# Two-block transformer kernel: one weight transfer behind the last shifted rows, mean sums split around the last taps, 64-column products in pairs, own rows read in runs

## Chip, cores and metric

The kernel runs on one core of a Trainium2 chip, as one program launched once. The metric is the time of one execution in microseconds (us), the median over several runs. The engines of the core are TensorE (PE, matrix products; its weight loads are PEld), VectorE (DVE), ScalarE (ACT), GpSimd (POOL) and SyncE (SP, which here only issues DMAs; POOL issues the indirect ones).

## The reference

The input x has 512 tokens of 1024 features. A first block has two layers, each a mixer and a convolutional FFN around residuals; the second layer's mixer is `conformer_conv`. A second block has a hybrid of attention and a state-space branch, a cross attention on a memory, and a mixture of 64 experts (8 per token) with a shared expert. What the change touches:

```python
def conformer_conv(x, pw1_w, pw1_b, dw_w, dw_b, ln_g, ln_b, pw2_w, pw2_b):
    h = jax.nn.glu(x @ pw1_w + pw1_b, axis=-1)
    h = causal_dwconv(h, dw_w, dw_b)             # 31 taps, each channel by itself
    h = jax.nn.silu(layer_norm(h, ln_g, ln_b))
    return h @ pw2_w + pw2_b

h_q, h_kv, k_rope_raw, u, g_mla, g_s5 = jnp.split(x @ w_in, IN_OFFSETS, axis=-1)
k_rope = apply_rope(k_rope_raw, cos, sin)        # 32 columns of w_in

scores = jax.nn.sigmoid((x2d @ w_router).astype(jnp.float32))   # 1024 -> 64 experts
...
return routed + swiglu(x2d, w_sh_gu, w_sh_down)  # then layer_norm_2(DEEPNORM_ALPHA * x + ff)
```

## The kernel before

Activations lie with features on the 128 partitions, as 8 tiles of 128 features by 512 tokens. Each engine has its own program, written out by hand in order; engines meet at semaphores. Weights come through a ring of two slots (`wring`), which SP fills in the order of its `slot(...)` calls (L745 to L755); one call issues two or three DMAs and waits until PE has used the slot's former content. Large products are split into high and low parts, three products for one (`proj_split`, L1405). Products of plain fp32 operands show in the profile as two PE instructions each.

**Depthwise convolution** (PE's `conv_taps`, L1685 to L1696). Of the 31 taps PE does 20 and DVE 11. For PE, a channel tile must lie in SBUF four times, shifted by 5 columns from one to the next. SP's `shift_rows(j)` (L856 to L864) makes these: one DMA writes the tile to DRAM (`conv_rows`, L858), and when that has landed, four DMAs read it back shifted (L864). For j >= 2 the reads also wait for the taps of tile j-2 (`tap_used`), whose buffer they fill. The 40 PE instructions of one tile (5 steps by 4 strips of 32 channels, 2 each) wait for these reads. The weights of the two pointwise products are six slots (`conv_slots`), issued between the tiles:

```python
for j in range(NK):
    shift_rows(j)
    if j % 2 == 0:
        slot(*conv_slots[2 + j // 2])
```

The layer norm behind it sums over features with a matrix of ones: `layer_norm` (L1491) adds the eight tiles into one PSUM bank, each once DVE has added its own taps (`conv_taken`); then `sum_squares` (L1473) does the same for the squares. DVE takes the mean at L3024. `keep_clock(n)` (L1353) issues n small products that nothing uses.

**Key product.** `tile` (L1361) multiplies the 64 columns `wkr` (the 32 rope key columns and the same ones turned for the rotation) with the 8 feature tiles; DVE multiplies by cosine and sine (L3507, `take_key`), and `spread_key` (L1755) adds the halves and repeats the key with a matrix `wrep` that POOL builds from the identity (L1201).

**Router.** After the second norm ACT writes the 8 tiles of `hT` (L2698), PE multiplies each with its 64 columns `wrt` (L2034), ACT copies the logits (L2798), and PE turns them to tokens on partitions (L2042). DVE's routing runs up to L3799, and PE's `positions` (L2053 to L2056) waits for its result. DVE also splits the shared expert's weights (`shared_lo`, L3750) and its inputs (L3761, L3762).

**Own rows.** The shared expert's down product goes to eight PSUM tiles of 128 tokens by 512 features. `own_row(i)` (L2153) first copies the tokens' residual rows there, as a product with the identity; `row_tok` holds a row with features in the order (k, q), and the tile wants (q, k). The first four `own_row` stand at the head, then `shared_down` (L2160 to L2162) with `m_idx` (L2084, an expert's token list) between, then the last four, one ahead of each further `shared_down`. DVE makes indices of the lists, POOL gathers the tokens of the first experts (L1279), and SP issues the first down weights of the experts (L1027) once the second gather has landed.

**Experts.** Per expert PE does 24 gate/up products (L2105 to L2107), transposes (L2093, L2115) and 12 down products (L2127 to L2129). ACT makes the high parts of the weights (gate/up L2836, down L2843) and DVE the low ones. SP loads three experts ahead, each load behind PE's last use of its buffer. The functions, as they were:

Of the kernel before, what the change touches and what calls it, by code (L numbers as in the profile page):

```python
# [28 lines left out]
ALU = mybir.AluOpType  # L29
ACT = mybir.ActivationFunctionType  # L30
AX = mybir.AxisListType

P = 128
T = 512
D = 1024
NK = D // P
# [113 lines left out]
def build(nc, A, out):  # L150

    ctx = ExitStack()
    with ctx:
# [73 lines left out]
        def align():  # L227

            top[0] = -(-top[0] // LINE) * LINE
# [337 lines left out]
        sc_c2 = carve(4 + 64)  # L567
        ranks = carve(TC * NE)
        align()
        sact_hi.append(carve_r(T)[1])  # L570
# [171 lines left out]
        def _(sp):  # L742
# [127 lines left out]
            for j in range(NK):  # L870
                shift_rows(j)
                if j % 2 == 0:
                    slot(*conv_slots[2 + j // 2])
            ffn(1)
# [251 lines left out]
        def _(pool):  # L1126
# [71 lines left out]
            pool.wait_ge(tile_done, IN_TILES)  # L1198
            for k in range(2):
                r = slice(32 * k, 32 * k + 32)  # L1200
                link(G.tensor_copy(wrep[r, :].rearrange("p (a b) -> p a b", b=32), ident[r, r].unsqueeze(1).broadcast_to([32, 4, 32])))  # L1201
# [128 lines left out]
        def _(pe):  # L1330
# [24 lines left out]
            def tile(mms, lo=0, hi=P, n=T):  # L1355
# [7 lines left out]
                tiles.inc()  # L1363

            def turn(srcs):

                b = tp[tiles.s % NBANK]
                if tiles.s >= NBANK:
                    pe.wait_ge(tile_evac, tiles.v - NBANK + 1)
                for k, src in enumerate(srcs):  # L1370
                    m = src.shape[0]
                    n = src.shape[1]
                    ins = nc.tensor.transpose(b[0:n, k * P:k * P + m], src, ident[0:m, 0:m])
                ins.then_inc(tile_done, 1)
                tiles.inc()
# [114 lines left out]

            def layer_norm(k, src, centred_sq):  # L1491
                for kk in range(k):
                    pe.wait_ge(conv_taken, kk + 1)
                    ins = nc.tensor.matmul(mp[0][:], ones[:], src[:, kk, :], start=kk == 0, stop=kk == k - 1)
                ins.then_inc(stat_ready, 1)
                nstat.inc()
                sum_squares(k, centred_sq, 1)

# [206 lines left out]
            for s in range(1, 4):  # L1705
                proj_split(NK, u_hi, u_lo, whi, (0, 2, 1, 3), each=lambda t: conv_between(s, t))
            conv_taps(NK - 2)
            conv_taps(NK - 1)
            layer_norm(NK, cv, lnsq)
            keep_clock(30)  # L1710
# [41 lines left out]
            def spread_key():  # L1752
                pe.wait_ge(key_turned, SINCE["key_turned"] + 1)
                pe.wait_ge(qstd, 2)
                nc.tensor.matmul(mp[1][:], wrep[0:64, :], turns[0:64, :], start=True, stop=True).then_inc(key_spread, 1)  # L1755

# [17 lines left out]
            pe.wait_ge(h_ready, NK)  # L1774
            tile([(wkr[:, k, :], hT[:, k, :]) for k in range(NK)], hi=64)
            for n in range(2):
# [254 lines left out]
            pe.wait_ge(in3, 16 * 4)  # L2031
            for k in range(NK):
                pe.wait_ge(h_ready, 3 * NK + k + 1)
                ins = nc.tensor.matmul(mp[2][0:NE, :], wrt[:, k, :], hT[:, k, :], start=k == 0, stop=k == NK - 1)  # L2034
            ins.then_inc(rt["logits"], 1)
            for c in range(TC):
                for half in range(2):
                    turn([hT[:, 4 * half + k, c * P:(c + 1) * P] for k in range(4)])
                if c == 0:
                    pe.wait_ge(rt["weights_hi"], 4 + 1)  # L2040
                    for c1 in range(TC):
                        ins = nc.tensor.matmul(mp[0][:, c1 * NE:(c1 + 1) * NE], logit_rows[0:NE, c1 * P:(c1 + 1) * P],  # L2042
                                               ident[0:NE, 0:NE], start=True, stop=True)
                    ins.then_inc(rt["logits"], 1)
# [108 lines left out]
            def own_row(i):  # L2153
                pe.wait_ge(tile_evac, RES_TILES - 8 + i - NBANK + 1)
                by_feature = row_tok[i // 2].rearrange("p (k q) -> p q k", k=NK)
                nc.tensor.matmul(down_bank(i), ident[:], by_feature[:, 64 * (i % 2):64 * (i % 2) + 64, :], start=True, stop=False)

# [80 lines left out]
        def _(act):  # L2238
# [558 lines left out]
            act.wait_ge(rt["logits"], 1)  # L2797
            nc.scalar.activation(logit_rows[0:NE, :], mp[2][0:NE, :], ACT.Copy).then_inc(rt["weights_hi"], 1)  # L2798
            act.wait_ge(rt["logits"], 2)
# [140 lines left out]
        def _(dve):  # L2940
# [562 lines left out]
            def take_key():  # L3503
                dve.wait_ge(sin_ready, 2)
                link(V.tensor_scalar(rope, rope, sc_consts[:, 1:2], None, ALU.mult))
                dve.wait_ge(tile_done, tiles.v + 1)
                link(V.tensor_tensor(turns[0:64, :], tp[tiles.s % NBANK][0:64, :], rope[0:64, :], ALU.mult))  # L3507
                dve.nop().then_inc(tile_evac, 1)
                dve.nop().then_inc(key_turned, 1)
                tiles.inc()  # L3510
# [236 lines left out]
            def shared_lo(c):  # L3747
# [3 lines left out]
                 .then_inc(rt["weights"], 1)  # L3751

            shared_lo(0)
            shared_lo(1)
# [295 lines left out]
```

## Time and profile before

| | us |
| --- | --- |
| median of 3 runs | 2661.35 (2660.39 to 2661.96) |
| the profiled execution | 2660.82 |
| its span in the trace | 2659.1 |
| PE busy | 2573.0 |
| DVE busy | 1922.9 |
| ACT busy | 1348.0 |
| POOL busy | 310.4 |

Times in the views count from the start of the span. A row of the timeline gives the start, the duration, the engine, the line of the kernel, the operation, output and inputs with their shapes, the number of instructions merged, and in brackets the idle time ahead of them with what ended it. The mean of PE's granted clock over the span is 0.992 of full speed.

### The profile page before, as it was taken

How to read it: one execution, taken by the hardware profiler on the slowest of the kernel's cores; microseconds unless marked ns; L12 is line 12 of the kernel's file. 1: busy time of each engine (PE TensorE's matmuls, PEld its weight loads, DVE VectorE, ACT ScalarE, POOL GpSimd, SP SyncE). 2: the span in 40 equal slices, each digit the busy share in tenths (PEclk: the TensorE clock that was granted, in tenths of full speed). 3: DMA queues.
4: the chain of work that ended last, by engine and by line, in shares of the span. 5: the costliest groups of instructions: out<-in, count | busy, mean ns of one | idle time of the engine just before them, and what ended most of it. 6: DMA issues, size and time to landing. Idle time of an engine off the chain costs nothing.

```text
span 2659.1 us, 34694 instructions
## 1 busy us (share of the span) xinstructions
PE 2573.0 (97%) x12396; PEld 1985.4 (75%) x12396; DVE 1922.9 (72%) x2762; ACT 1348.0 (51%) x1968; POOL 310.4 (12%) x270
## 2 busy tenths in 40 slices
PE   8999999999999989999999999999999999999996
PEld 7888878788887647888887765586667777777773
DVE  4788765677835856778637637465588999999996
ACT  4766652222323225222334233444457888998883
POOL 0000000100000010000002600000026622222220
PEclk9999999999999999999999999999999999999998
DMA  3222232222233651222233560323139999999996
GB/s 113 72 64 70 64 103 95 97 95 95 92 92 102 182 93 66 95 95 95 87 96 123 154 146 17 102 90 132 48 133 370 398 397 391 400 397 397 391 390 274
DMA packets 266488, 446.25 MB, mean 168 GB/s; under 512 B 46527, under 2 KB 200200, under 8 KB 241540
## 3 DMA queue, kind: packets, MB, share of 16 engines
q1 hardware_dynamic: 247555, 408.38, 43.9%
q0 software_dynamic: 18816, 36.35, 4.5%
q8 instruction: 70, 1.15, 0.2%
q14 instruction: 47, 0.38, 0.0%
HBM read 424.90 MB, written 44.84 MB: 177 GB/s over the span
## 4 chain that ended last, share of the span: by engine, by line
PE 87%; DVE 5%; DMA 3%; ACT 3%; issue 1%; SPq 1%; DVEq 0%; ACTq 0%
PE tp L1405 41%; PE tp L2105 4%; PE tp L2107 4%; PE tp L2106 4%; PE tp L1511 3%; PE tp L1513 3%; PE tp L1512 3%; PE tp L1361 2%; PE mp L2129 2%; PE mp L2127 2%; PE mp L2128 2%; PE tp L2093 2%; PE tp L1452 2%; PE mp L1694 1%; PE tp L1903 1%; DMA uT<-in_w_exp_gu 1%
## 5 line engine op out<-in xcount | busy, mean ns | idle before, releaser
L1405 PE MATMUL tp<-sq_r,arena_r 128*128 128x512 f32 x1056 | 414.3, 392 | 5.8 <-DVE uT_r L2986 3.5
L1405 PE MATMUL tp<-uT_r,arena_r 128*128 128x512 f32 x1056 | 411.9, 390 | 0.0
L1405 PE MATMUL tp<-sq_r,wring_r 128*128 128x512 f32 x1056 | 411.7, 390 | 0.0
L1405 PEld LDWEIGHTS tp<-sq_r,arena_r 128*128 128x128 f32 x1056 | 198.6, 188 | 55.1 <-issue 11.7
L1405 PEld LDWEIGHTS tp<-sq_r,wring_r 128*128 128x128 f32 x1056 | 198.7, 188 | 41.5
L1405 PEld LDWEIGHTS tp<-uT_r,arena_r 128*128 128x128 f32 x1056 | 198.7, 188 | 40.8 <-issue 0.5
L2958 DVE TENSOR_TENSOR wring_r<-wring,arena_r 128x2048 fp32r<-128x2048 f32 x82 | 187.2, 2322 | 50.1 <-ACT arena_r L2268 49.9
L1405 PE MATMUL tp<-arena_r,wring_r 128*128 128x512 f32 x564 | 219.5, 389 | 0.0
L2268 ACT ACTIVATE arena_r<-wring 128x2048 fp32r<-128x2048 f32 x82 | 152.2, 1903 | 52.4 <-DMA wring<-in_b_pw_w 21.9
L2511 ACT ACTIVATE arena<-arena 128x512 f32<-128x512 f32 x44 | 27.8, 632 | 288.1 <-DVE arena L3044 288.0
L3895 DVE TENSOR_TENSOR arena_r<-arena,arena_r 128x1024 fp32r<-128x1024 f32 x128 | 150.5, 1217 | 0.5 <-ACT arena_r L2843 0.5
L3044 DVE SCALAR_TENSOR_TENSOR arena<-lead,pcol,arena 128x512 f32<-128x512 f32 x176 | 132.4, 752 | 20.7 <-DVE arena L3044 4.9
L1405 PE MATMUL tp<-arena_r,sq_r 128*128 128x512 f32 x436 | 134.5, 390 | 0.0
L1405 PE MATMUL tp<-arena_r,uT_r 128*128 128x512 f32 x436 | 134.4, 390 | 0.0
L2255 ACT ACTIVATE lead<-tp 128x512 f32<-128x512 f32 x70 | 41.1, 597 | 175.7 <-PE tp L1405 126.2
L1511 PE MATMUL tp<-sq_r,wring_r 128*128 128x512 f32 x320 | 128.4, 401 | 0.9 <-DVE wring_r L3094 0.9
L2843 ACT ACTIVATE arena_r<-arena 128x1024 fp32r<-128x1024 f32 x128 | 127.8, 1049 | 0.0
L1513 PE MATMUL tp<-sq_r,wring_r 128*128 128x512 f32 x320 | 124.9, 390 | 0.0
L1512 PE MATMUL tp<-uT_r,wring_r 128*128 128x512 f32 x320 | 124.6, 389 | 0.0
L1405 PEld LDWEIGHTS tp<-arena_r,wring_r 128*128 128x128 f32 x564 | 105.9, 188 | 22.2
L2105 PE MATMUL tp<-hT_r,arena_r 128*112 128x512 f32 x256 | 103.1, 403 | 0.0
L3040 DVE TENSOR_TENSOR lead<-tp,rinv 128x512 f32<-128x512 f32 x88 | 60.6, 688 | 58.0 <-PE tp L1405 57.7
(625 smaller groups left out, 5950.3 us busy)
## 6 DMA issues: line engine op xcount, KB each, us to landing
wring<-in_w_exp_gu SPq DMA_DIRECT2D x64, 1024.0 KB, 14.5
arena<-in_w_exp_down SPq DMA_DIRECT2D x64, 1024.0 KB, 22.6
uT<-in_w_exp_gu SPq DMA_DIRECT2D x32, 1024.0 KB, 14.9
sq<-in_w_exp_gu SPq DMA_DIRECT2D x32, 1024.0 KB, 14.8
wring<-in_f_up_w SPq DMA_DIRECT2D x22, 1024.0 KB, 5.0
wring<-in_f_up_w SPq DMA_DIRECT2D x44, 512.0 KB, 6.3
wring<-in_f_down_w SPq DMA_DIRECT2D x32, 448.0 KB, 5.4
wring<-in_a_in_proj SPq DMA_DIRECT2D x42, 256.0 KB, 2.7
```

What stands on the lines that cost most here:

```text
L1405: ins = nc.tensor.matmul(b[:], parts[wp][:, kk, m * P:(m + 1) * P], xparts[xp][:, kk, :], start=n_k == 0 and q == 0, stop=n_k == k - 1 and ...
L1511: nc.tensor.matmul(bank[:], w_hi[:, kk, cs], u_hi[1][:, kk, :], start=kk == 0, stop=False)
L1512: nc.tensor.matmul(bank[:], w_hi[:, kk, cs], u_lo[1][:, kk, :], start=False, stop=False)
L1513: ins = nc.tensor.matmul(bank[:], w_lo[:, kk, cs], u_hi[1][:, kk, :], start=False, stop=kk == NK - 1)
L2105: nc.tensor.matmul(out, x_hi, hi[:, k, :], start=k == 0, stop=False)
L2106: nc.tensor.matmul(out, x_hi, lo[:, k, :], start=False, stop=False)
L2107: ins = nc.tensor.matmul(out, x_lo, hi[:, k, :], start=False, stop=k == NK - 1)
L2268: nc.scalar.activation(hi[r][1][:, a:b], wring[r][:, a:b], ACT.Copy).then_inc(whi_ready, 1)
L2843: nc.scalar.activation(wdn_hi[b][:, s], wdn[q][:, s], ACT.Copy).then_inc(moe["dhi"], 1)
L2958: V.tensor_tensor(wlo[r][:, a:b], wring[r][:, a:b], hi[r][1][:, a:b].bitcast(F32), ALU.subtract).then_inc(wlo_ready, 1)
L3044: ins = V.scalar_tensor_tensor(dst, r[:, PAD - t:PAD - t + T], w(taps - 1 - t), dst, ALU.mult, ALU.add)
L3895: V.tensor_tensor(wdn_lo[q][:, s], wdn[q][:, s], wdn_hi[b][:, s].bitcast(F32), ALU.subtract).then_inc(moe["dlo"], 1)
```

## The change

Four edits:

1. SP issues the last of the six weight slots behind `shift_rows(7)`, not behind `shift_rows(6)`.
2. PE does the first six mean sums between the taps of tile 6 and those of tile 7, and the last two behind those of tile 7.
3. The two products with 64 output columns (key and router) send even feature tiles to PSUM partitions 0 to 63 and odd ones to 64 to 127; the halves are added in what follows: `spread_key` contracts all 128 rows, and the logits' turn uses `two_idents`, two identities of 64 one above the other, which DVE makes. POOL builds four blocks of `wrep` in place of two. PE waits for `two_idents` ahead of the logits' turn.
4. `own_row` reads the residual row in runs of 64 contiguous numbers and writes PSUM in steps of 8 numbers (32 bytes), where it read in steps of 128 numbers (512 bytes) and wrote contiguously.

```diff
             for j in range(NK):
                 shift_rows(j)
-                if j % 2 == 0:
-                    slot(*conv_slots[2 + j // 2])
+                if j in (0, 2, 4, 7):
+                    slot(*conv_slots[2 + {0: 0, 2: 1, 4: 2, 7: 3}[j]])
...
-            for k in range(2):
+            for k in range(4):
                 r = slice(32 * k, 32 * k + 32)
...
+            def paired(bank, w, before):
+
+                for k in range(NK):
+                    before(k)
+                    half = bank[64 * (k % 2):64 * (k % 2) + 64, :]
+                    ins = nc.tensor.matmul(half, w[:, k, :], hT[:, k, :], start=k < 2, stop=k >= NK - 2)
+                return ins
...
-            def layer_norm(k, src, centred_sq):
-                for kk in range(k):
+            def conv_mean(ks):
+                for kk in ks:
                     pe.wait_ge(conv_taken, kk + 1)
-                    ins = nc.tensor.matmul(mp[0][:], ones[:], src[:, kk, :], start=kk == 0, stop=kk == k - 1)
-                ins.then_inc(stat_ready, 1)
-                nstat.inc()
-                sum_squares(k, centred_sq, 1)
+                    ins = nc.tensor.matmul(mp[0][:], ones[:], cv[:, kk, :], start=kk == 0, stop=kk == NK - 1)
+                return ins
...
             conv_taps(NK - 2)
+            conv_mean(range(NK - 2))
             conv_taps(NK - 1)
-            layer_norm(NK, cv, lnsq)
+            conv_mean(range(NK - 2, NK)).then_inc(stat_ready, 1)
+            nstat.inc()
+            sum_squares(NK, lnsq, 1)
...
-                nc.tensor.matmul(mp[1][:], wrep[0:64, :], turns[0:64, :], start=True, stop=True).then_inc(key_spread, 1)
+                nc.tensor.matmul(mp[1][:], wrep, turns, start=True, stop=True).then_inc(key_spread, 1)
...
-            tile([(wkr[:, k, :], hT[:, k, :]) for k in range(NK)], hi=64)
+            pe.wait_ge(tile_evac, tiles.v - NBANK + 1)
+            ins = paired(tp[tiles.s % NBANK], wkr, lambda k: None)
+            ins.then_inc(tile_done, 1)
+            tiles.inc()
...
-            for k in range(NK):
-                pe.wait_ge(h_ready, 3 * NK + k + 1)
-                ins = nc.tensor.matmul(mp[2][0:NE, :], wrt[:, k, :], hT[:, k, :], start=k == 0, stop=k == NK - 1)
-            ins.then_inc(rt["logits"], 1)
+            paired(mp[2], wrt, lambda k: pe.wait_ge(h_ready, 3 * NK + k + 1)).then_inc(rt["logits"], 1)
...
                     pe.wait_ge(rt["weights_hi"], 4 + 1)
+                    pe.wait_ge(rt["weights"], 1)
                     for c1 in range(TC):
-                        ins = nc.tensor.matmul(mp[0][:, c1 * NE:(c1 + 1) * NE], logit_rows[0:NE, c1 * P:(c1 + 1) * P],
-                                               ident[0:NE, 0:NE], start=True, stop=True)
+                        ins = nc.tensor.matmul(mp[0][:, c1 * NE:(c1 + 1) * NE], logit_rows[:, c1 * P:(c1 + 1) * P],
+                                               two_idents, start=True, stop=True)
...
             def own_row(i):
                 pe.wait_ge(tile_evac, RES_TILES - 8 + i - NBANK + 1)
-                by_feature = row_tok[i // 2].rearrange("p (k q) -> p q k", k=NK)
-                nc.tensor.matmul(down_bank(i), ident[:], by_feature[:, 64 * (i % 2):64 * (i % 2) + 64, :], start=True, stop=False)
+                by_slice = row_tok[i // 2].rearrange("p (k q) -> p k q", k=NK)[:, :, 64 * (i % 2):64 * (i % 2) + 64]
+                by_feature = down_bank(i).rearrange("p (q k) -> p k q", k=NK)
+                nc.tensor.matmul(by_feature, ident[:], by_slice, start=True, stop=False)
...
-            nc.scalar.activation(logit_rows[0:NE, :], mp[2][0:NE, :], ACT.Copy).then_inc(rt["weights_hi"], 1)
+            nc.scalar.activation(logit_rows, mp[2][:], ACT.Copy).then_inc(rt["weights_hi"], 1)
...
-                link(V.tensor_tensor(turns[0:64, :], tp[tiles.s % NBANK][0:64, :], rope[0:64, :], ALU.mult))
+                link(V.tensor_tensor(turns, tp[tiles.s % NBANK][:], rope, ALU.mult))
...
+            dve.wait_ge(in3, 16 * 4)
+            link(V.tensor_tensor(two_idents, ident[:, 0:NE], ident[:, NE:P], ALU.add))
             shared_lo(0)
```

On SP, at the last two tiles of the convolution, the order before was this (`conv_rows` is the buffer in DRAM, `arena` holds the shifted copies, `wring` is the ring of weights):

```order
L858 DMA conv_rows<-arena 128x542
L864 DMA arena<-conv_rows 32x4x516 x4
L752 DMA wring<-in_b_pw_w 128x3x512 x2
L752 DMA wring<-in_b_pw_w 128x2x512
L858 DMA conv_rows<-arena 128x542
L864 DMA arena<-conv_rows 32x4x516 x4
```

and now is this, with the three transfers of the last slot behind the reads of tile 7:

```order
L859 DMA conv_rows<-arena 128x542
L865 DMA arena<-conv_rows 32x4x516 x4
L859 DMA conv_rows<-arena 128x542
L865 DMA arena<-conv_rows 32x4x516 x4
L753 DMA wring<-in_b_pw_w 128x3x512 x2
L753 DMA wring<-in_b_pw_w 128x2x512
```

On PE, at the end of the same convolution, before (taps of tiles 5, 6 and 7 in one row, the means, the squares, and the products that nothing uses; a row of `order` counts products, of which the profile shows two instructions each):

```order
L1405 MATMUL tp<-sq_r,wring_r 128x512
L1694 MATMUL mp<-arena 32x512 x60
L1494 MATMUL mp<-arena,ones 128x512 x8
L1473 MATMUL mp<-arena,ones 128x512 x8
L1353 MATMUL mp<-ident 128x128 x30
```

and now, with six of the means ahead of the last 20 taps:

```order
L1414 MATMUL tp<-sq_r,wring_r 128x512
L1701 MATMUL mp<-arena 32x512 x40
L1503 MATMUL mp<-arena,ones 128x512 x6
L1701 MATMUL mp<-arena 32x512 x20
L1503 MATMUL mp<-arena,ones 128x512 x2
L1482 MATMUL mp<-arena,ones 128x512 x8
L1354 MATMUL mp<-ident 128x128 x30
```

On PE, at the first four own rows, before (ahead of them the shared expert's gate/up products, behind them its down products and an expert's list):

```order
L2068 MATMUL tp<-arena_r,wring_r 128x512
L2156 MATMUL tp<-arena,ident 128x512 x4
L2160 MATMUL tp<-hT_r,arena_r 128x512
L2161 MATMUL tp<-wring_r,arena_r 128x512
L2162 MATMUL tp<-hT_r,arena_r 128x512
L2084 MATMUL mp<-arena_r 128x6 x4
```

and now, in the same place, with the other shape of the access:

```order
L2079 MATMUL tp<-arena_r,wring_r 128x512
L2168 MATMUL tp<-arena,ident 128x8x64 x4
L2172 MATMUL tp<-hT_r,arena_r 128x512
L2173 MATMUL tp<-wring_r,arena_r 128x512
L2174 MATMUL tp<-hT_r,arena_r 128x512
L2095 MATMUL mp<-arena_r 128x6 x4
```

## Rows read from the trace of the kernel before

**Rows 1.** The page, first part: busy us, share of the span, instructions.
```profile
PE 2573.0 (97%) x12396; PEld 1985.4 (75%) x12396; DVE 1922.9 (72%) x2762; ACT 1348.0 (51%) x1968; POOL 310.4 (12%) x270
```
**Rows 2.** Chain of waits, 955 to 985 (start, us, what); then DVE's timeline.
```profile
955.09 8.62 DMA conv_rows<-arena
...
965.04 5.49 DMA arena<-conv_rows
...
976.84 7.08 PE mp L1494 x16
...
954.31 0.69 DVE L3342 TENSOR_TENSOR arena<-arena 128x512 f32<-128x512 f32 x1 [5.53 <-ACT arena L2255]
```
**Rows 3.** Timeline of PE at the last taps.
```profile
953.43 8.80 PE L1694 MATMUL mp<-arena 128*32 128x512 f32 x80
970.62 6.22 PE L1694 MATMUL mp<-arena 128*32 128x512 f32 x40 [8.40 <-DMA arena<-conv_rows]
```
**Rows 4.** Window behind the gap: us; busy PE, PEld, DVE, ACT, POOL; clock, DMA share, GB/s.
```profile
971.00:984.00 13.00, 12.90 (x56) 4.40 (x48) 0.75 (x2) 0.00 (x0) 5.53 (x7) 0.88 0.64 1
```
**Rows 5.** DMA issues, 934 to 950, then 950 to 976: KB, median us to landing.
```profile
conv_rows<-arena SPq DMA_DIRECT2D x1, 271.0 KB, 2.1
...
wring<-in_b_pw_w SPq DMA_DIRECT2D x1, 512.0 KB, 7.5
```
**Rows 6.** Timeline of ACT: first use of the moved slot.
```profile
1015.43 3.71 ACT L2268 ACTIVATE arena_r<-wring 128x2048 fp32r<-128x2048 f32 x2
```
**Rows 7.** Timeline of PE at the key product.
```profile
1465.71 7.08 PE L1361 MATMUL tp<-hT,arena 128*64 128x512 f32 x16
```
**Rows 8.** Timeline of POOL, first work behind the copies of L1201.
```profile
1446.69 1.70 POOL L1157 TENSOR_TENSOR arena<-pcol,arena 128x576 f32<-128x576 f32 x1 [37.08 <-ACT arena L2613]
```
**Rows 9.** Timelines of DVE, ACT, PE, DVE and PE at the router.
```profile
1930.76 2.36 DVE L3750 TENSOR_TENSOR wring_r<-wring,arena_r 128x1024 fp32r<-128x1024 f32 x2 [1.64 <-ACT arena_r L2788]
...
1937.88 5.36 ACT L2698 ACTIVATE hT<-sq,pcol 128x512 f32<-128x512 f32 x8 [2.32 <-DVE sq L3017]
...
1938.74 7.05 PE L2034 MATMUL mp<-hT,arena 128*64 128x512 f32 x16 [1.53 <-ACT hT L2698]
...
1963.31 0.29 DVE L3799 TENSOR_SCALAR arena<-arena 128x256 f32<-128x256 f32 x1
...
1963.97 0.33 PE L2054 MATMUL mp<-arena,stri 128*128 128x64 f32 x2
```
**Rows 10.** Chain of waits, 1976 to 2010; then the timelines of POOL and SP.
```profile
1978.18 6.91 PE tp L2156 x8
...
1992.43 1.81 PE tp L2156 x2
...
1995.62 1.73 PE tp L2156 x2
...
1992.34 1.51 POOL L1279 DMA_INDIRECT arena<-xtab,arena  x1 [0.30 <-issue]
...
1996.38 0.80 SPq L1027 DMA_DIRECT2D arena<-in_w_exp_down  x2
```
**Rows 11.** Windows before and in the experts' stage, columns as in rows 4.
```profile
1992.00:1996.30 4.30, 4.30 (x13) 2.10 (x14) 3.28 (x7) 1.20 (x2) 3.61 (x3) 1.00 0.23 65
...
2030.00:2600.00 570.00, 568.91 (x2838) 444.02 (x2837) 539.51 (x652) 500.29 (x727) 174.99 (x136) 1.00 1.02 396
```
**Rows 12.** Timeline of ACT in the experts' stage.
```profile
2419.73 3.90 ACT L2836 ACTIVATE hT_r<-sq 128x1024 fp32r<-128x1024 f32 x4 [1.85 <-DMA sq<-in_w_exp_gu]
```
**Rows 13.** Timeline of PE: one transpose, which comes once per expert.
```profile
2268.59 0.35 PE L2115 MATMUL mp<-ident,std 112*128 112x112 f32 x2
...
2416.00 0.35 PE L2115 MATMUL mp<-ident,std 112*128 112x112 f32 x2
...
2584.63 0.36 PE L2115 MATMUL mp<-ident,std 112*128 112x112 f32 x2
```
**Rows 14.** Chain of waits, 2585 to 2660, behind the last expert.
```profile
2598.99 20.72 DMA wring<-ytab
```

More of the change, by code:

```diff
@@ L568, in build @@
         ranks = carve(TC * NE)
+        two_idents = carve(NE)
         align()
```

## The prediction

> **What bounds the kernel now.** The page's first part [rows 1] comes first: TensorE (PE) is busy for 2573.0 of 2659.1 us. A step is therefore worth something if it takes time off PE's own queue or closes one of PE's few gaps, and work on another engine is worth something where PE, or the last stage, waits for it. Next, the chain of waits around the depthwise convolution [rows 2]: the last channel tile's DMA through DRAM takes 8.62 us, the reads of it end at 970.53 (965.04 + 5.49), and PE's 40 tap instructions begin only then, after 8.40 us of idleness; the mean sums follow and end at 983.92 (976.84 + 7.08), and VectorE (DVE) waits for them [rows 2, 3]. The windows give PE's granted clock behind this gap, from 971 to 984, as 0.88 on average [rows 4]: for a part of the stretch it had the lower of its two levels (1.2 and 2.4 GHz), after 8.4 us in which it did nothing. Third, the stage of the 64 experts. PE looks full there, but so are the DMA engines: 1.02 of their time, 396 GB/s, over 570 us [rows 11]. PE's timeline gives 16 experts in 2416.00 - 2268.59 = 147.41 us, 9.21 each, and the next 18 in 168.63 us, 9.37 each [rows 13]: late in the stage ScalarE (ACT) stands 1.85 us for an expert's weights [rows 12], which it did not earlier. From about 2416 on the transfers set the pace, and behind the last expert the chain is one transfer of 20.72 us [rows 14]. So a microsecond saved on PE just ahead of the experts counts only if it also lets the stream of transfers start earlier. The profiled execution took 2660.82 us; the median, 2661.35, is 0.53 above it, and I add that at the end.
>
> **The convolution's DMA order and its mean sums.** The data for the last tile are ready at 955.00 (954.31 + 0.69 on DVE [rows 2]), and its write is issued at once, but behind two weight transfers of 768 KB and one of 512 KB that SP issued just before. The same write took 2.1 us for the tile before it [rows 5]. With the weights moved behind, it lands at 955.1 + 2.1 = 957.2. The reads overwrite the rows of tile 5, whose taps end half way through the group of 80 instructions, at 953.43 + 4.40 = 957.83 [rows 3]; issued at 957.9, and taking from first issue to last landing what they took before (963.71 to 970.53, 6.8 us), they are in by 964.7.
> PE meanwhile ends the taps of tile 6 at 962.23 and does six of the eight means, 12 of the 16 instructions that take 7.08 us [rows 2]: 5.3 us, to 967.5. That is 2.8 us after the reads have landed. So the taps of tile 7 need no wait, and, with no gap ahead of them, take 4.4 us like those of tiles 5 and 6, not 6.22: to 972.0. Two means (1.8 us) end at 973.8. DVE's sum for tile 7 (0.7 us) lies beside the first of them. 983.9 - 973.8: **10.1 us earlier**, namely 8.4 of gap and 1.8 of slow taps, less 0.1. The moved slot issues three DMAs; they now start near 959.7 and land by about 967.5 (7.5 us [rows 5]). ACT first reads them at 1015.43 [rows 6], so nothing waits. On SP nothing else stands behind them until the FFN's weights.
>
> **The key product.** 16 instructions over 64 output columns take 7.08 us [rows 7], 0.44 each, one behind the other. The pairing puts neighbours on different halves of the array's columns. The taps do that with four strips of 32 columns: 80 instructions in 8.80 us, 0.11 each [rows 3], a quarter of 0.44. Two halves side by side should then give 0.22 each, 3.6 us. **Gain 3.4 us**, all on PE's queue. If they do not run side by side it is 0; nothing added could make it a loss. The sum of the two halves is folded into a product that now contracts 128 rows in place of 64: same number of columns, same time. GpSimd's two additional small copies lie in 37.08 us of idleness [rows 8]: 0.
>
> **The router's logits.** The same pairing on 16 instructions, 7.05 us [rows 9]. But ACT delivers their inputs until 1943.24 (1937.88 + 5.36), so the last pair can end only about 1944.3, 1.5 us earlier. Then DVE decides: its routing operations, which do not depend on this product's early end because the conversions of the inputs stand ahead of them in its queue, end at 1963.60 (1963.31 + 0.29), and PE's position sums wait for them at 1963.97 [rows 9]. PE arrives 1.5 us sooner and waits about 1.2: **gain 0.3 us**. The added sum of two identities on DVE (64 columns) falls into its 1.64 us of idleness ahead of 1930.76 [rows 9]: 0. The weights wait added on PE at the transposes is for that sum, long done.
>
> **The own rows.** Eight products, 16 instructions, copy the tokens' own rows into PSUM: 6.91 us for the first four, 1.81 + 3 x 1.73 for the others [rows 10] (two further groups read 1.73), 13.9 us, 0.86 per instruction, where a 128x512 product with contiguous operands takes 7.08/16 = 0.44. What differs is the read with a step of 512 bytes. The change reads runs of 64 contiguous numbers, and moves the step, 32 bytes, to the PSUM side. No row shows a stepped PSUM write by PE. Bounds: 0.44 as for contiguous operands, and 0.86 or above if the step costs there what it did on the read side. I take 0.44, because the taps and the mean sums, whose reads run without such steps, all stand at PE's streaming rate, and the one slow row has the one stepped read. Then PE saves 3.4 us on the first four and 6.8 us in all.
> The Trainium skill speaks against this: "PSUM — Partial Sum Buffer", section "Specifications (TRN2)", says that any non-contiguous access pattern there slows matmuls significantly, in cachelines of 8 bytes. By it the edit saves nothing and the time is that of the second rival below; no run shown here has such a write.
> What reaches the end is less. The expert indices and the gathers depend on the first four own rows alone; the gather of expert 1 is issued by GpSimd at 1992.34, and SP issues the first down weights behind its landing, 1996.38 [rows 10]. These move by 3.3 us; the DMA engines stand nearly idle there (share 0.23 from 1992 to 1996.3 [rows 11]). From then on they are full to the end, their work is unchanged, and the end follows them. **Gain 3.3 us**; the other 3.5 us come back as waits for weights, earlier in the stage than 2416.
>
> **Sum.** 10.1 + 3.4 + 0.3 + 3.3 = 17.1 us; 2660.82 - 17.1 = 2643.7, and with 0.53 the forecast is **2644.2 us**. A measurement of this kernel can tell about 0.2% (5.3 us) from no change.
>
> **Rivals.**
> 1. *The transfers keep up.* If a longer lead of PE only lengthens the queue of loads (their landing has grown without stopping PE until 2416), all 6.8 us count: 20.6 in all, 2640.8. Against it: 9.37 us an expert and ACT's waits at the end [rows 12, 13]. Chance 0.09.
> 2. *The step is as dear in PSUM as in SBUF.* The own rows stay at 0.86 and the other three give 13.8: 2660.82 - 13.8 + 0.53 = 2647.6. Every value between 0.44 and 0.86 lies between this and the forecast. For it: one stepped operand doubled the time in the row before. Chance 0.27.
> 3. *The pairs do not run side by side, or the reads of the last tile come late.* The first costs 3.4 + 0.3 (2647.9), the second what the reads land after 967.5: one more conflict like the 6.5 us that the write lost now would make it 3.7 us, 2647.9. The taps' 0.11 speaks against the one and the 2.8 us of slack against the other. Chance 0.09 together.
> 4. *The stepped PSUM write is far dearer*, the case on the slower side. With e us more per instruction than 0.86, PE is later by 16e and the transfers by 8e; PE has some 2.9 us in hand (18 x 0.16 us lost to the transfers). The gains are gone when 16e - 2.9 = 13.8, e = 1.04, 1.9 us per instruction, over four times a contiguous one. At 2.4 us (e = 1.54) it is 2660.82 - 13.8 + 21.7 + 0.53 = 2669.3. Nothing shows such a price. Chance 0.02 for slower by over 0.2%, and 0.05 for a price between, which leaves the time within 0.2%.
>
> **The numbers.** The forecast's own case has 0.48, with 1.5 us to either side for the windows that I read and the spread of the runs. The range takes in rivals 1 to 3, from 2640 to 2650; what is left out is rival 4 and two mishaps at once. Faster by over 0.2% means under 2656.0: cases 1 to 3 and the forecast, 0.93; within, 0.05; slower, 0.02.
>
> **What would show it.** Right: taps of tile 7 with no DMA wait and 4.4 us long, ahead of the last four mean instructions, and DVE taking the mean about 10 us sooner; 16 key instructions in about 3.6 us; logits ending about 1 us after ACT's last input and a new PE wait for DVE ahead of the position sums; own rows at 0.44; the down weights about 3.3 us sooner against the own rows' start, and ACT's waits for expert weights beginning well before 2350. Wrong: own rows at 0.86 or more (rival 2 or 4); 9.21 us an expert to the end (rival 1); a DMA wait still ahead of the last taps, or 0.44 a key instruction (rival 3).

## The result, and the profile after

| | before | changed |
| --- | --- | --- |
| median of 4 runs, us | 2661.65 | 2645.76 |
| lowest and highest, us | 2660.39, 2662.07 | 2645.16, 2646.24 |
| the profiled execution, us | 2660.82 | 2646.24 |
| its span, us | 2659.1 | 2644.5 |

The ratio is 0.9942, with a 95% interval of 0.9928 to 0.9956: 15.9 us faster by the medians, 14.6 us by the two profiled executions. The forecast was 2644.2 us, 17.1 us faster, in a range from 2640 to 2650. Of all runs below, one of e2_pairs took 3544.77 us at a mean granted clock of 0.68, and its median is that of its other ten.

The page's first part answers to [rows 1]; PE has lost 7.9 us of work:

```profile
PE 2565.1 (97%) x12396; PEld 1984.6 (75%) x12396; DVE 1921.5 (73%) x2763; ACT 1347.8 (51%) x1968; POOL 307.0 (12%) x272
```

PE's timeline at the end of the convolution, with DVE's step that takes the mean as the last line ([rows 2, 3]), and that step in the kernel before:

```profile
954.15 8.80 PE L1701 MATMUL mp<-arena 128*32 128x512 f32 x80
962.88 5.42 PE L1503 MATMUL mp<-arena,ones 128*128 128x512 f32 x12
968.23 4.50 PE L1701 MATMUL mp<-arena 128*32 128x512 f32 x40
972.66 2.00 PE L1503 MATMUL mp<-arena,ones 128*128 128x512 f32 x4
...
974.70 0.69 DVE L3036 TENSOR_SCALAR rinv<-mp 128x512 f32<-128x512 f32 x1 [1.22 <-PE mp L1503]
```
```profile
983.94 0.69 DVE L3024 TENSOR_SCALAR rinv<-mp 128x512 f32<-128x512 f32 x1 [6.35 <-PE mp L1494]
```

The last taps (x40) carry no bracket: they wait for nothing, and take 4.50 us where they took 6.22. The mean is taken 974.70 - 954.15 = 20.55 us behind the start of the group of 80, before 983.94 - 953.43 = 30.51.

What stands behind it is less good. PE's sums of squares, now and in the kernel before, and the windows there and ahead of the key product now (columns as in [rows 4]):

```profile
976.83 8.83 PE L1482 MATMUL mp<-arena,ones 128*128 128x512 f32 x16 [2.17 <-ACT arena L2332]
```
```profile
986.08 7.13 PE L1473 MATMUL mp<-arena,ones 128*128 128x512 f32 x16 [2.17 <-ACT arena L2320]
```
```profile
973.00:990.00 17.00, 14.83 (x61) 8.48 (x60) 9.62 (x12) 8.10 (x11) 5.53 (x7) 0.90 0.97 9
1450.00:1456.00 6.00, 4.24 (x16) 3.70 (x17) 5.97 (x5) 2.80 (x7) 5.84 (x3) 0.72 0.44 141
```

The same 16 instructions took 7.13 us in the kernel before, behind the same wait of 2.17 us, at a granted clock of 1.00. Here the clock was at its lower level (1.2 GHz of 2.4) for a part of each of the two stretches.

The key product, the router's logits and PE's wait ahead of the position sums ([rows 7, 9]):

```profile
1459.91 3.65 PE L1371 MATMUL tp<-hT,arena 128*64 128x512 f32 x16
...
1928.85 5.62 PE L1371 MATMUL mp<-hT,arena 128*64 128x512 f32 x16 [1.53 <-ACT hT L2710]
...
1953.75 0.43 PE L2065 MATMUL mp<-arena,stri 128*128 128x64 f32 x2 [1.13 <-DVE arena L3813]
```

The own rows in the chain of waits, and from the timelines of POOL and SP the second gather and the first down weights ([rows 10]):

```profile
1968.06 3.43 PE tp L2168 x8
...
1978.82 0.96 PE tp L2168 x2
...
1981.16 0.86 PE tp L2168 x2
```
```profile
1978.74 1.50 POOL L1280 DMA_INDIRECT arena<-xtab,arena  x1 [0.30 <-issue]
...
1984.30 0.80 SPq L1028 DMA_DIRECT2D arena<-in_w_exp_down  x2
```

Eight instructions in 3.43 us are 0.43 each. The experts' stage, a window, ACT's timeline and PE's transpose once per expert ([rows 11 to 13]), and ACT's first wait for weights in the kernel before:

```profile
2030.00:2580.00 550.00, 548.32 (x2722) 425.56 (x2721) 517.39 (x622) 483.36 (x703) 158.08 (x128) 1.00 1.02 396
```
```profile
2207.78 3.91 ACT L2848 ACTIVATE arena_r<-uT 128x1024 fp32r<-128x1024 f32 x4 [0.67 <-DMA uT<-in_w_exp_gu]
...
2233.12 0.35 PE L2126 MATMUL mp<-ident,std 112*128 112x112 f32 x2
...
2571.05 0.35 PE L2126 MATMUL mp<-ident,std 112*128 112x112 f32 x2
```
```profile
2353.49 3.91 ACT L2836 ACTIVATE arena_r<-wring 128x1024 fp32r<-128x1024 f32 x4 [0.35 <-DMA wring<-in_w_exp_gu]
```

The DMA engines move the same 396 GB/s. Apart from one wait of 1.09 us at 2028.85, ACT waits for an expert's weights from 2207.78 on, where the first such wait before stood at 2353.49. From 2233.12 the pace is lost: 36 experts in 337.93 us, 9.39 each, where [rows 13] has 9.21 up to 2416.

### The profile page after: what moved, and what is told of

Its sections match the earlier page's. It is cut to its first block, busy times and chain, and to the rows that moved or that the text cites. A ratio compares the mean times of both kernels' runs of the same rounds, so it can differ in the third digit from the quotient of the medians.

```text
span 2644.5 us, 34699 instructions
## 1 busy us (share of the span) xinstructions
PE 2565.1 (97%) x12396; PEld 1984.6 (75%) x12396; DVE 1921.5 (73%) x2763; ACT 1347.8 (51%) x1968; POOL 307.0 (12%) x272
## 4 chain that ended last, share of the span: by engine, by line
PE 86%; DVE 5%; DMA 4%; ACT 2%; SPq 1%; issue 1%; DVEq 0%; ACTq 0%; POOLq 0%
PE tp L1414 41%; PE tp L2116 4%; PE tp L2118 4%; PE tp L2117 4%; PE tp L1518 3%; PE tp L1520 3%; PE tp L1519 3%; PE tp L1362 2%; DMA uT<-in_w_exp_gu 2%; PE mp L2140 2%; PE mp L2138 2%; PE mp L2139 2%; PE tp L1461 2%; PE tp L2104 1%; PE mp L1701 1%; PE tp L1916 1%
```

## The experiments

All were timed beside the kernel before, whose medians in the three series were 2660.18, 2660.12 and 2660.38 us (21 runs each). A run strays by up to 4 us to either side, so differences between medians under 2 us are not read. The granted clock goes with the straying: of the 63 runs of the kernel before, the 16 with a mean clock of 0.990 or 0.991 average 2662.7 us, the four with 0.994 average 2657.0. The traces tell more, but each is of one execution, and not always a typical one: e6's is the fastest of its eleven runs (2649.85), e4's the second slowest (2659.64), e9's the slowest of five (2642.82), e10's the fastest (2642.94). The table cuts each profiled execution at rows of PE's and DVE's timelines: **A** from the start of the last full group of taps to DVE's mean, **B** from there to DVE's reciprocal behind the sums of squares, **C** from there to the key product, **D** from there to the position sums, **E** from the first own row to the end of the span. What lies ahead of A differs by up to 3.4 us between executions of whatever kernel (the taps start at 950.7 to 954.2). The traces of "before" and "changed", and the median of "changed", are those of the first comparison, whose median before is 2661.65.

| kernel | median, us | A | B | C | D | E |
| --- | --- | --- | --- | --- | --- | --- |
| before | 2660.2 | 30.51 | 10.02 | 471.74 | 498.26 | 681.07 |
| e1_conv | 2649.51 | 20.55 | 11.72 | 473.31 | 497.99 | 679.34 |
| e6_slot | 2654.55 | 23.44 | 10.03 | 471.71 | 498.20 | 679.65 |
| e7_means | 2655.77 | 25.05 | 10.02 | 473.34 | 498.38 | 680.79 |
| e2_pairs | 2657.31 | 30.28 | 11.72 | 473.41 | 494.23 | 679.63 |
| e3_own | 2655.91 | 30.12 | 11.72 | 473.24 | 498.22 | 674.66 |
| e4_first | 2657.71 | 30.26 | 11.72 | 473.28 | 498.12 | 676.95 |
| e5_last | 2658.22 | 30.54 | 10.02 | 471.70 | 498.31 | 677.88 |
| changed | 2645.76 | 20.55 | 11.72 | 473.49 | 493.83 | 676.62 |
| e10_again | 2644.55 | 20.55 | 11.72 | 473.37 | 494.37 | 674.38 |
| e8_fill | 2641.93 | 20.55 | 10.02 | 471.80 | 494.18 | 675.38 |
| e9_down | 2640.92 | 20.55 | 11.72 | 473.39 | 494.14 | 675.91 |
| e11_down0 | 2641.71 | 20.55 | 11.72 | 473.40 | 494.57 | 674.40 |
| e12_best | 2642.65 | 20.55 | 10.03 | 471.80 | 494.55 | 674.83 |

The first comparison read by it: 0.72 ahead of A, -9.96 in A, +1.70 in B, +1.75 in C, -4.43 in D, +0.10 up to the own rows, -4.45 in E: -14.6 us, the difference of the spans. E holds also what stands behind the last expert's activation on ACT, 58.4 to 60.1 us, in which the clock drops as well (0.81 from 2600 to 2659 in the kernel before): 60.1 us in the kernel before and 59.1 in the changed one, so 1.0 of the 4.45 us lies there.

### The parts by themselves

**e1_conv**: the kernel before with the two convolution edits.

```diff
-                if j % 2 == 0:
-                    slot(*conv_slots[2 + j // 2])
+                if j in (0, 2, 4, 7):
+                    slot(*conv_slots[2 + {0: 0, 2: 1, 4: 2, 7: 3}[j]])
...
             conv_taps(NK - 2)
+            conv_mean(range(NK - 2))
             conv_taps(NK - 1)
-            layer_norm(NK, cv, lnsq)
+            conv_mean(range(NK - 2, NK)).then_inc(stat_ready, 1)
```

> The two convolution edits alone (weight slot behind the last shifted rows, six means ahead of the last taps). In the changed kernel DVE takes the mean 974.70 - 954.15 = 20.55 us behind the start of the last full group of taps, before 983.94 - 953.43 = 30.51 us: 9.96 us. Behind it the granted clock was 0.90 from 973 to 990, where the kernel before had 1.00 in the like stretch, and DVE's next step stands only 8.25 us ahead. Theory 1: that slower clock belongs to the edit, because PE now meets its 2.17 us wait for the squares in another state: about 2653.4 us (8.3 faster than 2661.65), and the profile shows a clock under 1.00 behind the mean sums. Rival: it was chance of the one execution: about 2651.7 us (10 faster), clock 1.00 there.

Measured: 2649.51 us, ratio 0.9958 (0.9945 to 0.9972), 10.7 us faster by the medians; the interval holds both sums expected (8.3 and 10), so the time does not tell the theories apart. A is 9.96 us shorter; B and C carry the 1.7 us each, and the window behind the mean sums reads a clock of 0.90:

```profile
969.00:986.00 17.00, 14.83 (x60) 8.27 (x57) 9.30 (x11) 8.10 (x11) 5.53 (x7) 0.90 0.94 9
```

But e2, e3 and e4, whose convolution is that of the kernel before, carry both too (e3's sums of squares below). So the slower clock does not need the edit, and theory 1 falls, though its sign, a clock under 1.00, is there. The one execution of the kernel before that the forecast was read from happened to have neither.

```profile
984.40 8.83 PE L1473 MATMUL mp<-arena,ones 128*128 128x512 f32 x16 [2.17 <-ACT arena L2321]
```

**e2_pairs**: the kernel before with the paired key and router products and what follows them.

```diff
-            tile([(wkr[:, k, :], hT[:, k, :]) for k in range(NK)], hi=64)
+            pe.wait_ge(tile_evac, tiles.v - NBANK + 1)
+            ins = paired(tp[tiles.s % NBANK], wkr, lambda k: None)
...
+            paired(mp[2], wrt, lambda k: pe.wait_ge(h_ready, 3 * NK + k + 1)).then_inc(rt["logits"], 1)
```

> The paired key and router products alone, with the two identities and the 128-row followers. Theory: 7.08 us become 3.65 us at the key, 0.3 us are gained at the router, nothing is given back later: 3.7 us faster, about 2657.9 us. In the changed kernel the 24 products ahead of the key took 6.28 us, before 5.47, at a granted clock of 0.72 from 1450 to 1456: if the pairing brings that slower clock, the gain is about 2 us, 2659.7; if the shift of what stands ahead brings it, the clock is 1.00 here. Rival: the POOL copies or DVE's wide step delay something and the gain is under 2 us with the clock at 1.00.

Measured: 2657.31 us, ratio 0.9985 (0.9976 to 0.9995), 2.9 us by the medians. D, which holds both products, is 494.23, 4.0 us under the 498.2 of the seven kernels without the pairs. C is 473.41, and its slow clock stands at about 1418, far ahead of the key product: the pairing does not bring it.

**e3_own**: the kernel before with the own rows read in runs.

```diff
-                by_feature = row_tok[i // 2].rearrange("p (k q) -> p q k", k=NK)
-                nc.tensor.matmul(down_bank(i), ident[:], by_feature[:, 64 * (i % 2):64 * (i % 2) + 64, :], start=True, stop=False)
+                by_slice = row_tok[i // 2].rearrange("p (k q) -> p k q", k=NK)[:, :, 64 * (i % 2):64 * (i % 2) + 64]
+                by_feature = down_bank(i).rearrange("p (q k) -> p k q", k=NK)
+                nc.tensor.matmul(by_feature, ident[:], by_slice, start=True, stop=False)
```

> The own rows' edit alone. PE's time on them falls from 13.9 to 7.0 us. Theory 1 (the transfers set the end of the experts' stage): the stage's transfers start only about 2 to 3.4 us sooner, so the kernel is about 3.3 us faster, 2658.3 us, and ACT's waits for expert weights begin well before 2350. Rival (PE sets it): 6.8 us faster, 2654.9 us, and 9.21 us an expert to the end.

Measured: 2655.91 us, ratio 0.9985 (0.9976 to 0.9994), 4.3 us by the medians, between the two sums; the interval, 1.6 to 6.4 us, leaves out the rival's 6.8. From ACT's timeline: the first expert's activation comes 27.1 us behind the first own row, before 34.1, so PE has its 7.0 us there; the last expert's comes 616.0 behind, before 621.0. The stage of the experts, first to last activation, is 588.9 us against 586.9, and ACT waits for weights from 2274.65 on (before 2353.49):

```profile
2274.65 3.91 ACT L2837 ACTIVATE arena_r<-wring 128x1024 fp32r<-128x1024 f32 x4 [0.31 <-DMA wring<-in_w_exp_gu]
```

**e10_again**: the changed kernel a second time.

> The changed kernel once more, beside the kernels of this call. The three parts by themselves gave 10.7, 2.4 and 4.3 us, 17.4 in sum. If they add, about 2660.2 - 17.4 = 2642.8 us; if what was lost in the first comparison (15.9 us) belongs to the parts being together, 2644.3 us. The profile also shows whether the slower clock ahead of the key product and behind the mean sums comes again.

Measured: 2644.55 us, ratio 0.9942 (0.9929 to 0.9956), 15.6 us. The three parts sum to 17.8 by the medians (the expectation's 2.4 and 17.4 count all eleven runs of e2); a gap of 2.2 us lies within their intervals. Both slow clocks came again, the second at about 1410 in place of 1452, behind two other waits of PE for DVE (1.30 and 1.81 us). So the place of the second one, next to the key product or before it, differs between two executions of one kernel. ACT's steady waits for weights begin at 2244.08 here, and PE's pace of 9.21 us an expert breaks at 2278.

### The two convolution edits apart

**e6_slot**: the slot alone. **e7_means**: the split means alone.

```diff
-                if j % 2 == 0:
-                    slot(*conv_slots[2 + j // 2])
+                if j in (0, 2, 4, 7):
+                    slot(*conv_slots[2 + {0: 0, 2: 1, 4: 2, 7: 3}[j]])
```
```diff
             conv_taps(NK - 2)
+            conv_mean(range(NK - 2))
             conv_taps(NK - 1)
+            conv_mean(range(NK - 2, NK)).then_inc(stat_ready, 1)
```

> The last weight slot behind the last shifted rows, and nothing else. Theory: the reads of tile 7 land about 9.9 us behind the start of the last full group of taps, some 1.1 us behind its end instead of 8.4; then 4.4 us of taps and 7.1 of means, so DVE takes the mean about 21.5 us behind that start, where it was 30.5: 9 of the 10 us are this edit's, about 2651 us against 2660.2 before. Rival: the gap is only shortened and PE's clock stays low behind it, so that taps and means are slow: mean at 24 us or later.

> Six means ahead of the last taps, and the slot where it was. Theory: the reads still land 17.1 us behind the start of the group of taps, the means fill 5.3 us of the gap, and only taps (4.4 to 6.2 us) and two means (1.8 us) follow: mean taken at 23.5 to 25.3 us, 5 to 7 us gained, about 2654 us against 2660.2 before. So the two edits overlap: by themselves 9 and 6, together 10. Rival: the means ahead are free of the gap's cost only if the clock recovers; if not, under 4 us gained.

Measured: 2654.55 us (0.9980, 0.9971 to 0.9989) and 2655.77 us (0.9985, 0.9976 to 0.9994). PE's timelines, of the slot alone and of the means alone:

```profile
951.04 8.80 PE L1694 MATMUL mp<-arena 128*32 128x512 f32 x80
962.88 4.50 PE L1694 MATMUL mp<-arena 128*32 128x512 f32 x40 [3.04 <-DMA arena<-conv_rows]
```
```profile
959.85 5.42 PE L1494 MATMUL mp<-arena,ones 128*128 128x512 f32 x12
968.41 5.79 PE L1692 MATMUL mp<-arena 128*32 128x512 f32 x40 [3.14 <-issue]
974.13 2.00 PE L1494 MATMUL mp<-arena,ones 128*128 128x512 f32 x4
```

With the slot alone the reads land 11.8 us behind the start of the group (962.88 - 951.04), not 9.9: I had taken the landing of one read for that of the four, which are issued one behind the other; the forecast's 11.3 (964.7 - 953.43) was nearer. The gap is 3.04 us, A gains 7.07 where 9 was expected, and the taps run at full speed. With the means alone A gains 5.46, as expected, and the taps are slow behind the gap that is left. The edits overlap: 7.1 and 5.5 by themselves, 9.96 together. The means fill what is left of the gap.

### What the own rows are worth

**e4_first** and **e5_last**: the kernel before with the own rows' edit on rows 0 to 3, or on rows 4 to 7.

```diff
+                if i < NBANK:
                     by_slice = row_tok[i // 2].rearrange("p (k q) -> p k q", k=NK)[:, :, 64 * (i % 2):64 * (i % 2) + 64]
...
+                else:
                     by_feature = row_tok[i // 2].rearrange("p (k q) -> p q k", k=NK)
```
```diff
+                if i >= NBANK:
```

> The own rows' edit on the first four rows alone; the last four keep the read with the 512-byte step. PE saves 3.4 us instead of 6.8. Theory (the transfers set the end): the first down weights are issued as early as with all eight rows, so the gain is that of the whole edit, 4.3 us as measured with all eight (2655.9 us against 2660.2 before). Rival (PE sets the end): half of the whole.

> The own rows' edit on the last four rows alone. PE again saves 3.4 us, but behind the point from which the gathers and the first down weights follow. Theory (the transfers set the end): no gain beyond 0.7 us, about 2660 us, and the stage of the experts is longer by what PE came early. Rival (PE sets the end): 3.4 us faster, about 2656.8 us.

Measured: 2657.71 us (0.9987, 0.9978 to 0.9996) and 2658.22 us (0.9991, 0.9982 to 1.0), 2.4 and 1.9 us by the medians. E is 676.95 and 677.88 against a mean of 680.1 for the five kernels with the old own rows: 3.1 and 2.2 us; all eight rows give 4.9 (mean of seven, 675.2). Up to the last expert's activation alone it is 2.8, 1.5 and 4.5 us. So neither theory holds as I put it. All of PE's 6.8 us do not arrive, but the last four rows are not worthless. The timeline of SP with the last four alone shows what they moved: the first down weights stand 18.4 us behind the first own row, as before, but expert 3's gate/up weights, which wait for the last tile of the own rows' stage, come at 2002.81, 25.8 us behind it, where they came 29.2 us behind (2007.23 - 1978.02).

```profile
1995.41 0.80 SPq L1027 DMA_DIRECT2D arena<-in_w_exp_down  x2
...
2002.81 1.09 SPq L1020 DMA_DIRECT2D wring<-in_w_exp_gu  x2
```

From the traces' DMA records, 150 MB are moved 387.6 to 387.9 us behind the first own row in the five executions with the old own rows, 384.65 with the first four, 385.54 with the last four, and 382.3 to 384.1 (mean 383.4) in the seven with all eight: 3.0, 2.1 and 4.3 us, beside 3.1, 2.2 and 4.9 in E. So the end moves with the transfers, and two releases move them, not one. That PE's own lead adds nothing to it is not shown by these runs.

**e9_down**: the changed kernel, the first down weights behind the first gather. **e11_down0**: one of the two ahead of the wait.

```diff
-            sp.wait_ge(gathered[1], 16)
+            sp.wait_ge(gathered[0], 16)
             expert_down(0, 0)
```
```diff
-            sp.wait_ge(gathered[1], 16)
             expert_down(0, 0)
+            sp.wait_ge(gathered[1], 16)
             expert_down(1, 1)
```

> The changed kernel, with the first two down weights issued behind the first gather's landing and not the second's, about 5 us sooner; PE's program is untouched. Theory (the transfers set the end): the stream of transfers starts sooner, its idle stretch ahead of the down weights closes, and the kernel is 3 to 5 us faster than the changed kernel beside it. Rival 1 (PE sets the end): within 0.7 us of the changed kernel. Rival 2: the second gather now lands behind 2 MB of weights, some 5 us later, and PE's transposes of expert 1 wait for it: slower than the changed kernel, or no gain.

> The changed kernel with the first down weight (1 MB) issued directly behind the gate/up weights, ahead of the wait for the second gather. The transfers then have no idle stretch there (2.9 us in the changed kernel), and the first two gathers land about 2.6 us later, which PE's transposes of experts 0 and 1 meet as a wait of up to 1 us. Theory (the transfers set the end): 2 to 3 us faster than the changed kernel (2644.5 in the call before, 15.6 under the kernel before), although PE loses up to 1 us there. Rival (PE sets the end): up to 1 us slower than it.

Measured: 2640.92 us (0.9925, 0.9911 to 0.9938) and 2641.71 us (0.9935, 0.9922 to 0.9949). The medians are 3.6 and 2.8 us under e10_again. The three intervals against the kernel before overlap, but e9 ran in one series with e10, and all its five runs (2640.06 to 2642.82) lie under all of e10's (2642.94 to 2646.84). That this is the edit's doing is not shown: the runs of e9 had a mean granted clock of 0.994, those of e10 0.992, and by the traces neither edit did what it was meant to. In e9 SP issues the down weights 15.75 us behind the first own row, the changed kernel 16.40 and 16.12. The first gather, issued at 1971.40, takes 9.5 us to land, the second 5.5 (DMA issues, windows 1971 to 1973 and 1975 to 1977):

```profile
arena<-xtab,arena POOLq DMA_INDIRECT x1, 9.5
...
arena<-xtab,arena POOLq DMA_INDIRECT x1, 5.5
```

Both land when the 4 MB of gate/up weights ahead of them are through: the last of these at 1980.71, the gathers at 1980.92 and 1981.54. In e11 the first down weight does go out at once, but the second, and the stores behind it, wait for the second gather until 18.4 us behind the first own row, and the idle stretch only moves: in the 34 us from the first own row, no packet of 2 KB or more is under way for 2.6 us in all, by the DMA records, against 2.8 in both executions of the changed kernel (1.9 in e9, 5.4 in the kernel before). E, 675.91 and 674.40, is within the 674.4 to 676.6 of the others. So this test of the transfers' theory is void; it rests on e3 to e5, and on what e8 and e12 show below.

### The slower clock

**e8_fill**: the changed kernel with unused products in two gaps. **e12_best**: with e11's edit besides.

```diff
             conv_mean(range(NK - 2, NK)).then_inc(stat_ready, 1)
             nstat.inc()
+            keep_clock(9)
...
+                    if t == 2:
+                        keep_clock(8, mp[0])
                     turn_inputs(t - 1)
```

> The changed kernel, with unused products in two gaps of PE: 9 (about 2.1 us) between the mean sums and the sums of squares, 8 (about 1.9 us) ahead of the transposes that wait for DVE before the key product. Theory 1: the slower clock behind these two gaps costs 1.7 us each, and with the gaps filled the granted clock stays 1.00 there: 2645.8 - 3.4 = 2642.4 us. Rival: the time is lost otherwise, or the drop in the clock comes from idleness further ahead: 2645.8 us within 0.7, or slower by up to 1 us if a filler outlasts its gap.

> The changed kernel with both gaps of PE filled by unused products (as before in this study) and the first down weight ahead of the gather's wait. If both gains stand: about 2660.2 - 18.3 - 2.5 = 2639.4 us. If the fillers' gain was chance: about 2642 us.

Measured: 2641.93 us (0.9932, 0.9918 to 0.9946) and 2642.65 us (0.9936, 0.9923 to 0.9950). PE's timeline of e8 and the window, which in the changed kernel read 0.90:

```profile
974.31 2.17 PE L1354 MATMUL mp<-ident 128*128 128x128 f32 x18
976.64 7.13 PE L1482 MATMUL mp<-arena,ones 128*128 128x512 f32 x16 [0.16 <-ACT arena L2335]
```
```profile
973.00:990.00 17.00, 16.84 (x96) 11.99 (x95) 11.31 (x14) 9.38 (x13) 5.40 (x7) 1.00 0.96 9
```

With the gap filled the squares take 7.13 us. B is 10.02 and 10.03 in the two filled kernels, and 11.72 in all five with both convolution edits and the gap open. By two executions against five, the slow clock of B comes from that gap, and the filler takes it away. C is 471.80 in both filled kernels too, though the wait at 1410 behind which the clock fell in e10 was not filled. C was slow in all eight executions with a slow B, and in one of the other four with the gap open (e7, whose clock had fallen at the last taps); why the second drop goes with the first is open.

The two filled executions, and no other, have a new drop: the clock reads 0.57 from 1994 to 1998, at the first experts. PE's tenth expert (its transpose as in [rows 13]) then stands 119.2 and 119.9 us behind the first own row, 117.2 in e10. E is longer than e10's 674.38 by 1.0 and 0.5 us only, so half or more of PE's delay there does not reach the end, as the transfers' theory has it; a hint only, as E differs by 2.2 us between the two executions of the changed kernel.

By the medians e8 is 2.6 us under e10_again and e12 1.9, intervals overlapping; the traces show 3.3 us in B and C. e12 came out where it was expected if the fillers' gain was chance. That any of the four variants is faster than the changed kernel for its edit's sake is not shown.

## Why the prediction was right

**The convolution.** 10.1 us forecast, 9.96 in A, each link as written: no wait ahead of the last taps, 4.50 us of taps, the mean two short instructions behind. It is right for the reason given, and e6 and e7 show that both edits are needed for it. What it lacked is B and C: the forecast took the mean's shift to the end unchanged, and did not look at the 2.17 us wait behind it, where the clock may fall. The kernel before pays that too in three of five executions with its convolution, so on the average the change loses about 1.3 us by it, and not the 3.4 us of the first comparison.

**The key and the router.** 3.65 us forecast to be 3.6, and a new PE wait for DVE of 1.13 us ahead of the position sums, forecast 1.2: 3.7 us in the forecast, 4.0 in D.

**The own rows.** The stepped PSUM write costs nothing that shows: 0.43 us per instruction, the bound that was taken. The Trainium skill's rule ("PSUM — Partial Sum Buffer", section "Specifications (TRN2)"), that a non-contiguous pattern slows matmuls significantly, does not hold for this write of 512 numbers in steps of 32 bytes: the measurement decides, and rivals 2 and 4 fall with it. That the transfers take back a part of PE's 6.8 us was right, with the signs named: waits of ACT for weights from 2207.78, the pace lost at 2233 in place of 2416. In e10 these stand at 2244 and 2278. Rival 1 (all 6.8) falls. The step that was mis-sized is "**Gain 3.3 us**; the other 3.5 us come back": by E it is 4.9, and 4.5 up to the last expert's activation. Two errors are in it. The down weights came only 2.0 us sooner against the first own row (18.36 to 16.40; 2.2 in e10, 3.0 in e3), since the second gather, which lands behind gate/up weights, took 5.56 us (1978.74 to 1984.30), not 4.0. And the last four rows do move transfers, those of expert 3 and of the down weights behind it, worth 2.2 us in e5.

**The sum.** By the segments: 9.96 + 4.0 + 4.5 to 4.9, less 1.3 to 3.4 us of slower clock, is 15.1 to 17.5, against 15.9 and 15.6 measured. The forecast of 17.1 was near partly because two errors, the own rows' and the clock's, stood against each other.

## What to carry to other kernels

Where a stage is busy on PE and on DMA alike, ask of each microsecond saved ahead of it which transfers it releases sooner, all of them and not only the first: here 4.9 of PE's 6.8 us reached the end, beside 4.3 us by which the transfers were ahead. Bulk loads issued ahead of a small dependent transfer can set that transfer's landing as well: in e9 the two gathers behind 4 MB of weights landed 0.2 and 0.8 us after the last of them. And read a stretch with short waits in more than one execution before its time goes into a sum: the clock behind the same 2.17 us wait was full in some executions and not in others.

## What the runs showed that I had not expected

A step of 512 bytes on the side that PE reads doubles an fp32 product (0.86 us against 0.44), a step of 32 bytes on the side that it writes to PSUM leaves it at 0.43. Two 64-column products on the two halves of the array take 0.23 us each (3.65/16), about half of the 0.44 that one takes alone. A wait of 2.17 us on PE was followed by a lower clock in eight of the twelve profiled executions in which it stood open, at 1.70 us each time; nine products that nothing uses, 2.17 us long, kept it at full there in both executions that had them. In these two, and in none of the others, it fell at 1994.
